# Prompt sliding-window attention moved from a stage of its own into the weight tiles of the mLSTM projection, in eight half-size units, with two bank pairs for those tiles

## The reference

```python
sq, sk, sv, mq, mk, mv, mo, mi, mf = split_cols(h @ w_in, EVEN_SIZES)
sq = rope(rmsnorm(sq.reshape(bsz, t, SW_HEADS, SW_HEAD_DIM), q_norm), pos, SW_ROT_DIM, ROPE_THETA)
sk = rope(rmsnorm(sk.reshape(bsz, t, SW_KV_HEADS, SW_HEAD_DIM), k_norm), pos, SW_ROT_DIM, ROPE_THETA)
...
# swa_prompt, blocks of 128 queries against their own and the previous block of keys
scores = jnp.einsum('bnqkgd,bnskd->bnkgqs', qb, kk) * (SW_HEAD_DIM ** -0.5)
p = sink_probs(scores, valid, sink)
o = jnp.einsum('bnkgqs,bnskd->bnqkgd', p, vv)
...
y = jnp.concatenate([ya.astype(h.dtype), hb.astype(h.dtype)], axis=-1) @ w_out
```

## Time and profile before

| | before |
|---|---|
| median of three runs | 2006.59 us (2002.33 to 2008.85) |
| profiled execution, its span | 2007.15 us, 2005.4 us |
| PE busy | 1778.0 us, 89% |
| DVE busy | 839.9 us, 42% |
| ACT busy | 606.9 us, 30% |
| POOL busy | 587.9 us, 29% |
| mean granted clock of PE | 0.909 of full speed |

### The profile page before, as it was taken

How to read it: one execution, slowest core, us unless ns; L and a number is a source line. 1 busy time by engine, 2 the same in 40 slices (tenths; PEclk the granted TensorE clock), 3 DMA queues, 4 the chain that set the end, 5 groups by cost and what they waited for, 6 DMA issues and landing times.

```text
span 2005.4 us, 31352 instructions
## 1 busy us (share of the span) xinstructions
PE 1778.0 (89%) x13456; PEld 1666.0 (83%) x13456; DVE 839.9 (42%) x1209; ACT 606.9 (30%) x1038; POOL 587.9 (29%) x260
## 2 busy tenths in 40 slices
PE   6896685997899999999899977866898799999997
PEld 5895464896799999999899955755787699999997
DVE  4445456453532121226865244659572442111211
ACT  3233311343343232322341211315433343232311
POOL 1330000331144444443443300002242044444442
PEclk9997675998999999999999976668998999999999
DMA  4221001253143333332233221315145033333332
GB/s 122 75 82 48 22 22 45 69 177 123 44 120 96 95 91 89 96 95 76 74 96 85 79 57 42 85 32 148 43 137 189 17 100 96 95 88 93 95 95 75
DMA packets 294044, 170.64 MB, mean 85 GB/s; under 512 B 18839, under 2 KB 281159, under 8 KB 293754
## 3 DMA queue, kind: packets, MB, share of 16 engines
q1 hardware_dynamic: 253016, 123.85, 22.2%
q10 hardware_dynamic: 40890, 44.79, 7.0%
HBM read 155.91 MB, written 13.84 MB: 85 GB/s over the span
## 4 chain that ended last, share of the span: by engine, by line
PE 78%; DVE 11%; ACT 4%; issue 2%; DMA 2%; ACTq 1%; SPq 0%; POOL 0%; DVEq 0%; POOLq 0%
PE banks L377 21%; PE banks L379 20%; PE banks L378 20%; PE banks L864 1%; PE banks L713 1%; PE banks L1751 1%; ACT w_hi L427 1%; PE banks L1776 1%; DMA w_raw<-in_mem_wo 1%; PE banks L2488 1%; PE banks L1792 1%; PE banks L2609 1%; DVE norm_acc L312 1%; PE banks L682 1%; PE banks L2568 1%
## 5 line engine op out<-in xcount | busy, mean ns | idle before, releaser
L438 POOL TENSOR_TENSOR w_lo<-w_raw,w_hi 128x1024 fp32r<-128x1024 f32 (+2 forms) x256 | 587.7, 2296 | 1392.6 <-ACT w_hi L427 1392.6
L377 PE MATMUL banks<-xn_hi,w_hi 128*128 128x260 f32 (+1 forms) x1920 | 549.8, 286 | 15.8 <-issue 12.0
L379 PE MATMUL banks<-xn_hi,w_lo 128*128 128x260 f32 (+1 forms) x1920 | 545.2, 284 | 0.0
L378 PE MATMUL banks<-xn_lo,w_hi 128*128 128x260 f32 (+1 forms) x1920 | 543.5, 283 | 0.0
L427 ACT ACTIVATE w_hi<-w_raw 128x1024 fp32r<-128x1024 f32 (+2 forms) x256 | 252.7, 988 | 915.1 <-PE banks L379 862.6
L377 PEld LDWEIGHTS banks<-xn_hi,w_hi 128*128 128x128 f32 (+1 forms) x1920 | 361.0, 188 | 18.4 <-issue 12.6
L378 PEld LDWEIGHTS banks<-xn_lo,w_hi 128*128 128x128 f32 (+1 forms) x1920 | 360.6, 188 | 1.4
L379 PEld LDWEIGHTS banks<-xn_hi,w_lo 128*128 128x128 f32 (+1 forms) x1920 | 360.7, 188 | 0.8
L379 PE MATMUL banks<-hid_hi,w_lo 128*128 128x260 f32 x1024 | 289.4, 283 | 0.0
L377 PE MATMUL banks<-hid_hi,w_hi 128*128 128x260 f32 x1024 | 289.2, 282 | 0.0
L378 PE MATMUL banks<-hid_lo,w_hi 128*128 128x260 f32 x1024 | 288.4, 282 | 0.0
(11 more groups left out here) (477 smaller groups left out, 2556.0 us busy)
## 6 DMA issues: line engine op xcount, KB each, us to landing
w_raw<-in_ffn_w SPq DMA_DIRECT2D x128, 512.0 KB, 4.0
w_raw<-in_odd_w_in SPq DMA_DIRECT2D x36, 512.0 KB, 3.7
kc<-in_cache_mem_k ACTq DMA_DIRECT2D x16, 512.0 KB, 8.3
vc<-in_cache_mem_v ACTq DMA_DIRECT2D x16, 512.0 KB, 9.4
w_raw<-in_even_w_in SPq DMA_DIRECT2D x14, 512.0 KB, 3.7
w_raw<-in_odd_w_out SPq DMA_DIRECT2D x24, 256.0 KB, 2.7
...
```

What stands on the lines that cost most here:

```text
L377: pe.matmul(out, hi[:, kk, 0:m], r, start=kk == 0, stop=False)
L378: pe.matmul(out, hi[:, kk, 0:m], q, start=False, stop=False)
L379: last = pe.matmul(out, lo[:, kk, 0:m], r, start=False, stop=kk == nk - 1)
L438: pool.tensor_tensor(k.w_lo[n % RING][:, view[0], view[1]], k.w_raw[n % RING][:, view[0], view[1]], k.w_hi[n % RING][:, view[0], view[1]]. ...
```

## The change

- The stages `EvenTurn` and `SwaPrompt` are gone from the list. Their work hangs on tiles 7 to 18 of the even projection. For that PE can take a step inside a tile, ahead of chunk kk (`inside`).
- The attention is done in eight units (a block of 128 queries, half the heads: 4). Unit u has its scores in tile 8+u ahead of chunk 0, its transposes in tile 9+u ahead of chunk 4 and its products with the values ahead of chunk 7. Scores lie in banks 4 and 5, transposes and results in 6 and 7. The tiles of this projection therefore use two bank pairs (banks 0 to 3), so PE waits before tile n for the copy out of tile n-2.
- The ten transposes of `EvenTurn`: three (values, last key block, sample) in tile 8, the seven for the mLSTM in tiles 16 to 18. The six output DMAs are issued by ACT behind tile 9.
- `QueryKeyNorm` starts at tile 1 instead of 5 and takes one tile per chunk instead of two: the sum for chunk c in tile 2+c ahead of chunk 5, the rotation in tile 3+c ahead of chunk 4, and DVE's product and its three rotation operations both behind tile 2+c.
- The attention's result goes to `xa_hi`/`xa_lo`, the mLSTM's to `ym`; the output matmul reads its rows from the one and then the other. The number of its matmuls is the same.

```diff
-            if n >= 3:
-                pe.wait_ge(k.tile_out.s, n - 2)
+            if k.last_in_pair[n] >= 0:
+                pe.wait_ge(k.tile_out.s, k.last_in_pair[n] + 1)
...
+                for step in t.get(("pe_at", kk), ()):
+                    step(pe)
...
+def bank_pairs(tiles):
+
+    pair_of, last_in_pair, last = [], [], {}
+    for n, t in enumerate(tiles):
+        pair_of.append(n % t.get("pairs", 3))
+        last_in_pair.append(last.get(pair_of[n], -1))
+        last[pair_of[n]] = n
+    return pair_of, last_in_pair
...
+def inside(tiles, i, kk, step):
+
+    tiles[i].setdefault(("pe_at", kk), []).append(step)
...
-            i = first + 2 * c
+            i = first + c
             follow(tiles, i, None, lambda act, n, c=c: self.act_square(act, c))
-            follow(tiles, i + 2, pe=lambda pe, c=c: self.pe_sum(pe, c))
-            follow(tiles, i + 1, None, lambda act, n, c=c: self.act_rstd(act, c))
-            follow(tiles, i + 2, lambda dve, n, c=c: self.dve_norm(dve, c))
-            follow(tiles, i + 5, pe=lambda pe, c=c: self.pe_rotate(pe, c))
-            follow(tiles, i + 4, lambda dve, n, c=c: self.rope.dve_apply(dve, c))
+            follow(tiles, i, None, lambda act, n, c=c: self.act_rstd(act, c))
+            inside(tiles, i + 1, 5, lambda pe, c=c: self.pe_sum(pe, c))
+            follow(tiles, i + 1, lambda dve, n, c=c: self.dve_norm(dve, c))
+            inside(tiles, i + 2, 4, lambda pe, c=c: self.pe_rotate(pe, c))
+            follow(tiles, i + 1, lambda dve, n, c=c: self.rope.dve_apply(dve, c))
...
-    qk = QueryKeyNorm(k, tiles, 5)
+    for t in tiles:
+        t["pairs"] = 2
+    qk = QueryKeyNorm(k, tiles, 1)
     qk.tile0 = len(k.tiles) + 1
+    even_turns(k, tiles, SwaPrompt(k, tiles, 8, qk.rope))
...
+    for i in range(3):
+        inside(tiles, 8, 1 + 2 * i, lambda pe, i=i: pairs.pe_item(pe, i))
+    follow(tiles, 7, lambda dve, n: pairs.dve_item(dve, 0))
+    follow(tiles, 7, None, lambda act, n: pairs.act_item(act, 1))
+    follow(tiles, 7, lambda dve, n: pairs.dve_item(dve, 2))
+    for u in range(2 * NBLK + 1):
+        swa.unit(tiles, u)
+    follow(tiles, 9, None, store)
...
+    def unit(self, tiles, u):
+
+        t, units = self.first + u, 2 * NBLK
+        if u:
+            follow(tiles, t - 1, lambda dve, n: self.dve_probs(dve, u - 1), lambda act, n: self.act_turned(act, u - 1))
+            inside(tiles, t, 4, lambda pe: self.pe_turn(pe, u - 1))
+            inside(tiles, t, 7, lambda pe: self.pe_values(pe, u - 1))
+        if u < units:
+            inside(tiles, t, 0, lambda pe: self.pe_scores(pe, u))
+            follow(tiles, t - 1, lambda dve, n: self.dve_max(dve, u), lambda act, n: self.act_exps(act, u))
+        if u:
+            follow(tiles, t - 1, lambda dve, n: self.dve_out(dve, u - 1))
...
-    s += [EvenTurn(k), SwaPrompt(k), SwaSample(k), even_spread(k)]
-    k.mid.reset(8 * TOK * 4)
+    s += [SwaSample(k), even_spread(k)]
+    k.mid.reset()
+    k.ym = tuple(k.mid(f"ym_{n}", [P, 4, TOK], F32R) for n in ("hi", "lo"))
```

More of the change, by code:

```diff
@@ L704, in __init__, with pe_item @@
         k.turn_count += len(items)
[L706 to L714 removed]
+    def pe_item(self, pe, i):
+        k, pieces = self.k, self.items[i][0]
+        if i >= self.ring:
+            pe.wait_ge(self.free.s, self.base + i - self.ring + 1)
+        for src, c0 in pieces:
+            rows, n = src.shape
+            last = pe.transpose(k.ps[0:n, self.bank + i % self.ring, c0:c0 + rows], src, self.ident(src, rows))
+        last.then_inc(self.done.s, 1)
+    def pe(self, pe):
+        for i in range(len(self.items)):
+            self.pe_item(pe, i)
     def ident(self, src, rows):
@@ new lines, in even_turns, with first @@
+    items = [(turn4(E_MK + j), four, k.mk_tok[:, :, j * P:j * P + P]) for j in range(2)]
+    items += [(turn4(E_MV + h), four, k.mv_tok[:, :, h, 0:P]) for h in range(4)]
+    items.append(([(p[:, E_MV + h, SEQ:TOK], h * P) for h in range(4)], lambda b: b[0:8, 0:512], k.mv_s[:, :]))
+    memory = Turn(k, "ml_turn", items, 4, 2)
+    def first(pe):
+        pe.wait_ge(swa.masked.s, 2 * NBLK)
+        memory.pe_item(pe, 0)
+    inside(tiles, 16, 1, first)
+    for i, kk in ((1, 16 * 8 + 6), (2, 17 * 8 + 1), (3, 17 * 8 + 3), (4, 17 * 8 + 6), (5, 18 * 8 + 1), (6, 18 * 8 + 4)):
+        inside(tiles, kk // 8, kk % 8, lambda pe, i=i: memory.pe_item(pe, i))
@@ new lines, in even_turns, with __init__ @@
+    follow(tiles, 14, lambda dve, n: dve.memset(k.mv_tok[:, :, :, P:P + 1], 1.0))
+    for i, t in ((0, 15), (2, 16), (4, 16), (6, 17)):
+        follow(tiles, t, lambda dve, n, i=i: memory.dve_item(dve, i))
+    for i, t in ((1, 15), (3, 16), (5, 17)):
+        follow(tiles, t, None, lambda act, n, i=i: memory.act_item(act, i))
+class SwaPrompt:
+    def __init__(self, k, tiles, first, rope):
+        self.k, self.first, self.rope = k, first, rope
+        k.big.reset(20 * TOK * 4)
+        k.sv_tok = k.big("sv_tok", [P, NBLK, P])
+        k.mk_tok = k.big("mk_tok", [P, NBLK, 2 * P])
+        k.mv_tok = k.big("mv_tok", [P, NBLK, 4, P + 1])
@@ L1038, in pe_scores, with keys @@
+    def keys(self, u):
+        return max(u // 2 - 1, 0)
+    def pe_scores(self, pe, u):
+        k, ps, p, n, kb = self.k, self.k.ps, self.k.proj, u // 2, self.keys(u)
+        if u:
+            pe.wait_ge(self.masked.s, u)
+        else:
+            pe.wait_ge(self.rope.done.s, self.rope.base + 5)
+        for g in range(2):
             for v in range(2):
-                rows, at = slice(64 * v, 64 * v + 64), 256 * (g % 2)
-                last = pe.matmul(ps[:, 2 * v + g // 2, at:at + 256], p[rows, g, n * P:n * P + P],
+                rows = slice(64 * v, 64 * v + 64)
+                last = pe.matmul(ps[:, 4 + v, 256 * g:256 * g + 256], p[rows, 2 * (u % 2) + g, n * P:n * P + P],
@@ new lines, in pe_values @@
+    def pe_values(self, pe, u):
+        k, ps, kb = self.k, self.k.ps, self.keys(u)
+        pe.wait_ge(self.pt_ready.s, u + 1)
+        for g in range(2):
+            for v in range(2):
+                for s in range(2):
+                    last = pe.matmul(ps[64 * v:64 * v + 64, 6, g * P:g * P + P],
+                                     k.sv_tok[:, kb + s, 64 * v:64 * v + 64], self.pt[:, g, 2 * v + s, :],
+                                     start=s == 0, stop=s == 1)
+        last.then_inc(self.pv.s, 1)
@@ L1114, in act_exps @@
+    def act_exps(self, act, u):
+        i = u % 2
+        act.wait_ge(self.max_ready.s, u + 1)
+        for h in range(4):
             act.activation(self.s[i][:, h, :], self.s[i][:, h, :], ACT.Exp, scale=0.125, bias=self.nm[i][:, h:h + 1],
```

245 lines of the change are left out of this document (96 added, 149 removed).

## The result

The changed kernel takes 1987.66 us (median of 4 runs, 1980.94 to 1990.90) against 2007.72 for the kernel before; the ratio is 0.9908 [0.9882, 0.9934]. Measured again beside other kernels it is 1986.60 against 2004.13, ratio 0.9908 [0.9892, 0.9924]. So it is faster by 17.5 to 20 us by these medians, not by 29.9. The profiled execution took 1989.41 us (span 1987.6), 17.7 less than the one before.

What follows compares the result with a forecast made beforehand. PE, busy 89% of the span, was read as the bound, idling or slow in EvenTurn and SwaPrompt. Removing 72.75 us, less 28.0 added work and 14.9 more stalls, nets 29.9: from 2007.15 to 1977 us, range 1968 to 1989.

Steps and rivals of the forecast that it cites:

- The 72.75 us: Time from EvenTurn's first transpose to SwaSample's first matmul, 159.60 to 232.35, forecast to leave the path.
- the first hole: In tile 3, PE's chunk 0 rotation waits for DVE's norm product behind dve_running: 10.8 us, plus 1.7 for slow clock.
- the second is 3.47: Second hole, in tile 4: PE waits for chunk 1's norm behind dve_exponents, with POOL holding up DVE: 3.6 us.
- unit 0 is late once: Unit 0's maximum stands on DVE behind the sample's transposes of tile 8: a PE stall of 1.6 us.
- the third bank pair: Projection tiles wait for the copy out of tile n-2, done early enough, so a third pair was not needed.
- the switch: A ready insertion in a tile costs PE only its matmul spacing, nothing for switching; 2.98 us per attention unit.
- the part behind the change: The rest of the program has the same instructions, no change in time; SwaSample could gain 0 to 2 us, taken as 0.
- every other tile to pay: When POOL starts before DVE's division, PE waits 0.95 us; in every other tile, 3.3 us for seven, bounds 0 and 6.6.
- an even chance of another 1.7: PE's clock may drop after the wait for chunk 1's norm in tile 4, costing 1.7 us; put at 0.9.
- the second (1985 us): Rival: a unit's chain binds its tiles, POOL in every tile +3.3, DMAs +2, slow clock +3; 1985 us, chance 0.20.
- the six DMAs: ACT's output DMAs behind tile 9 delay tile 12's high part some 3 us, still ready; uncovered, up to 4 us.
- The first rival: DVE and POOL don't meet, or DVE is always first: 6.5 us better, 1971 us, chance 0.18.

Runs made afterwards that it cites:

- runs with POOL held: Changed kernel, POOL's low part waiting for the unit's division (tiles 10 to 17) and the gate exponents (tile 5); 1977.18 and 1975.30 us.
- the combination with POOL held: Changed kernel with gate arithmetic in five pieces, unit 0's maximum before the sample's copy, and POOL's low part waiting for divisions in tiles 10 to 17; 1971.68 us.
- the 12 runs with the idle time: Changed kernel plus 21 ACT copies (about 22 us) between the projection and SwaSample; 2008.78 us, ratio 1.0020 to the kernel before.
- the two experiments without the units: Kernel before with two bank pairs: 2004.51 us; the same plus norm and rotation from tile 1, one tile per chunk: 2016.71 us.
- the spread gates alone: Changed kernel with the gate arithmetic in five pieces behind tiles 2 to 6, each after that tile's norm and rotation; 1968.14 us.
- the scores done twice: Changed kernel with each unit's scores computed twice into the same place; 1988.37 us in one run.
- the spread gates with late values: Changed kernel with gate arithmetic in five pieces, unit 0's maximum before the sample's copy, and values products one tile later beside the next scores; 1968.65 us.

## Why the prediction was right and wrong

Right: the mechanism and the sign. The 72.75 us left; the first hole is 10.70 us for a forecast of 10.8, with DVE's norm product as its releaser; the second is 3.47 for 3.6; L1325 and the cosine product (L711, 0.69 us) are free of POOL; unit 0 is late once; the third bank pair was spare; the clock is 1.00 in the attention's tiles.

Wrong: the time, 1987.7 for 1977. In the profiled executions 12.2 us are missing, 6.3 up to SwaSample and 5.9 behind its start. The two largest terms are two that the sum put at nothing: the switch ("nothing for the switch"), which measured 3.6 us in eight units, and the part behind the change ("the rest of the program has the same instructions"), 5.9 us. Up to SwaSample:

- "So an insertion that is ready costs its spacing, here 0.89 us, and nothing for the switch." This was read off the sums of the earlier trace rows, which are full matmuls like the tile's own. The scores use 64 rows and the values 64 columns of the array, and cost 1.26 and 1.27 us instead of 1.00 and 1.01, while the transposes cost 0.87 instead of 0.97. The runs with POOL held put a unit at 3.43 us, not 2.98: 8 x 0.45 = 3.6 us. The largest error ahead of SwaSample.
- "I expect every other tile to pay, 3.3 us for seven." POOL was first in every tile but the one with the output DMAs. The tile then lasts as long as the meeting makes it, so the same tie comes again a tile later; the late exponentials that should have turned it around did not: they ended 0.15 us before PE was through with the tile (ACT's small one at 151.17 took 0.19, PE's next scores start at 151.52), so ACT's high part was not late. 5 x 0.78 (9.94 - 9.16) + 1.39 us ahead of unit 7's transposes = 5.3 us: 2.0 more.
- "This one has an even chance of another 1.7" for the clock. From one rotation to the next takes 7.50 us where nothing is awaited (for example 52.02 to 59.52 in the combination with POOL held). Here it was 62.93 to 76.22 = 13.29, less the wait of 3.47 is 9.82: the clock's loss behind the first hole is 2.3 us, not 1.7. From 76.22 to 85.44 it is 9.22, so 1.7, not 0.9. Together 1.4 more. Windows of PE alone (length, busy, granted clock, DMA) show both:

```profile
62.90:66.50 3.60, 3.57 (x11) 0.50 0.00 0
66.50:76.20 9.70, 6.25 (x46) 0.96 0.16 42
76.20:79.80 3.60, 3.58 (x15) 0.68 0.11 33
```

- Unit 0's wait was 1.03 instead of 1.6, and the holes 0.2 shorter: 0.8 less.

That is 3.6 + 2.0 + 1.4 - 0.8 = 6.2 of 6.3 us.

Behind SwaSample's start the other 5.9 us are missing (23.6 there, 17.7 at the end). "The rest of the program has the same instructions" is true, and its time was not the same. It varies from run to run: over the 17 runs of the kernel before it is 1767 to 1777 us, over the 12 runs with the idle time 1772 to 1782. But its median is 1771.8 in the one and 1777.4 in the other, 1774 to 1776 in the two experiments without the units, and 1776.6 to 1783.5 in the versions with them but one (the spread gates alone, three runs). In the profiles the lead of the changed kernel, by the start of the same DVE instruction, is (times of the kernel before) 25.4 us at 236, 22.7 at 250, 24.0 at 1290, 21.9 at 1320, 21.0 at 1502 and 17.7 from 1585 on. Three places make up most of the loss:

- SwaSample. The prediction put its start at 0. The full clock at its beginning won 1.8 us and the wait for the cache's load took 2.64, so the transposes come 0.9 us later (7.96 for 7.09).
- The stretch from 1290 to 1320, 2.1 us. PE alone (length, busy, granted clock, DMA), before and then after, the same 156 matmuls:

```profile
1290.00:1320.00 30.00, 23.55 (x156) 0.78 0.00 1
```

```profile
1266.00:1298.00 32.00, 25.72 (x156) 0.69 0.00 1
```

PE is 2.17 us longer busy with them at the lower clock, which is the whole loss of this stretch.
- The stretch from 1502 to 1585, 3.3 us. PE is busy 65.77 us instead of 64.42 with the same 454 matmuls, at clock 0.85 instead of 0.87; the other 2.0 us is time in which PE idles, and what it waits for more was not traced.

Between these places the lead grows by 1.3 us (250 to 1290) and falls by 0.9 (1320 to 1502). So about 3.5 us of what is lost is PE's clock in stages that the change doesn't touch, and 0.9 a load that lands later; what held the load up was not tested. In the 13 profiles the stretch from 1290 to 1320 takes either 30.0 to 30.6 us or 32.2 to 32.5. The short group has the kernel before and both experiments without the units, but also the scores done twice and the spread gates with late values; so the units don't settle it. The idle stage put back ahead of SwaSample did not bring the time back, so density just ahead of it is not the cause; what decides the clock there stays open.

On the rivals: the second (1985 us) comes nearest in time, and half of its mechanism is there, the meeting in nearly every tile. But the chain of a unit didn't bind: with POOL held the tiles are bare work, and with the scores done twice no wait is left in tiles 10 to 15. The other parts of its price did not come either: the six DMAs held ACT's high part up by 1.42 us without a wait of PE, and by that made the one division free, and the clock's loss behind the longer hole was 0.6 us more, not 3. The first rival was tested by the POOL runs: without the meeting it is 10 us faster, where the prediction had priced it at 6.5; the clock behind the second hole, which the prediction had at 0.9, measured 1.7, and every tile but one paid.

The Trainium skill, page "SBUF — State Buffer", section "Who interferes with whom", says that the instruction which comes second at the shared port of VectorE and GpSimd waits for the whole length of the first. The runs agree down to the smallest operation here, 0.15 us that became 2.34 (L1377), and in both orders (POOL, second at 116.52, took 2.96 us). Taking the meeting away took the wait away in three places: the gate exponents, the divisions and the norm products.
